# Second attention of a two-layer encoder trunk: all projections first, then the units, then one output projection

## The reference

```python
def chunk_band_mixer(h, w_in, q_g, k_g, rel_table):
    proj = h @ w_in                       # 1024 -> 3 * 1024
    q, k, v = jnp.split(proj, 3, axis=-1) # 16 heads of 64
    q = rmsnorm(q.reshape(B, S, N_HEADS, HEAD_DIM), q_g)
    k = rmsnorm(k.reshape(B, S, N_HEADS, HEAD_DIM), k_g)
    ...
    # per 64-frame chunk: its own chunk and the 8 before it
    logits = jnp.einsum('bqhd,bkhd->bhqk', q_c, k_c) * HEAD_DIM ** -0.5 + bias
    logits = jnp.where(valid, logits, -jnp.inf)
    p = jax.nn.softmax(logits, axis=-1)
    o = jnp.einsum('bhqk,bkhd->bqhd', p, v_c)
```

## Time and profile before

| | |
|---|---|
| median of 3 runs | 3090.85 us (3089.18 to 3092.53) |
| profiled execution: time, span | 3089.12 us, 3087.3 us |
| granted clock of PE, mean | 0.960 |
| PE busy over the span | 2810.6 us, 91% |
| PEld | 2390.3 us, 77% |
| DVE | 1702.2 us, 55% |
| ACT | 1042.0 us, 34% |
| POOL | 790.8 us, 26% |

### The profile page before, as it was taken

How to read it: one execution, slowest core, us unless ns; L and a number is a source line. 1 busy time by engine, 2 the same in 40 slices (tenths; PEclk the granted TensorE clock), 3 DMA queues, 4 the chain that set the end, 5 groups by cost and what they waited for, 6 DMA issues and landing times. The chain is left out here.

```text
span 3087.3 us, 38817 instructions
## 1 busy us (share of the span) xinstructions
PE 2810.6 (91%) x14642; PEld 2390.3 (77%) x14674; DVE 1702.2 (55%) x2824; ACT 1042.0 (34%) x1912; POOL 790.8 (26%) x417
## 2 busy tenths in 40 slices
PE   5879498999899999999888888888887999999999
PEld 4679387888788888888777877777776888888887
DVE  4689766661444444444556555556566544445444
ACT  4567455551322222222333332333334222222221
POOL 2031433302332232322231111121102322232322
PEclk9989699999999999999989999999998999999999
DMA  4010000011111111111010000000001111111111
GB/s 158 1 62 21 21 8 8 5 59 35 68 54 44 48 50 45 54 48 48 36 43 5 29 33 33 33 1 33 13 8 55 55 48 48 41 54 41 54 48 62
DMA packets 36310, 124.09 MB, mean 40 GB/s; under 512 B 3968, under 2 KB 12336, under 8 KB 34384
## 3 DMA queue, kind: packets, MB, share of 16 engines
q1 hardware_dynamic: 36176, 122.29, 11.4%
HBM read 118.03 MB, written 9.49 MB: 41 GB/s over the span
## 5 line engine op out<-in xcount | busy, mean ns | idle before, releaser
L330 PE MATMUL banks<-XH,WH 128*128 128x512 f32 x1408 | 436.2, 391 | 8.2 <-POOL WL L291 6.1
L330 PE MATMUL banks<-XL,WH 128*128 128x512 f32 x1408 | 434.8, 390 | 0.0
L330 PE MATMUL banks<-XH,WL 128*128 128x512 f32 x1408 | 434.6, 390 | 0.0
L291 POOL TENSOR_TENSOR WL<-WR,WH 128x1024 fp32r<-128x1024 f32 x132 | 331.0, 2515 | 370.3 <-ACT WH L245 370.3
L386 DVE TENSOR_TENSOR U<-banks,RB 128x1024 f32<-128x1024 f32 x88 | 107.8, 1225 | 407.4 <-PE banks L330 398.1
L260 ACT ACTIVATE Y<-U,CONVB,CONVW 128x1024 f32<-128x1024 f32 x88 | 109.5, 1245 | 633.0 <-DVE U L386 633.0
L330 PEld LDWEIGHTS banks<-XH,WH 128*128 128x128 f32 x1408 | 265.0, 188 | 64.8 <-POOL WL L291 6.3
L330 PEld LDWEIGHTS banks<-XL,WH 128*128 128x128 f32 x1408 | 265.1, 188 | 55.3
L330 PEld LDWEIGHTS banks<-XH,WL 128*128 128x128 f32 x1408 | 265.1, 188 | 55.3
L376 DVE TENSOR_TENSOR XT<-XT,banks 128x1024 f32<-128x1024 f32 x176 | 214.4, 1218 | 165.2 <-PE banks L346 165.2
L299 POOL TENSOR_TENSOR AL<-Y,AH 128x1024 fp32r<-128x1024 f32 x44 | 105.8, 2405 | 611.3 <-ACT AH L268 611.3
(11 more groups left out here) (217 smaller groups left out, 5624.8 us busy)
## 6 DMA issues: line engine op xcount, KB each, us to landing
WR<-in_ffn SPq DMA_DIRECT2D x132, 512.0 KB, 3.2
QWR<-in_qkv SPq DMA_DIRECT2D x12, 1536.0 KB, 7.4
XT<-in_xT SPq DMA_DIRECT2D x16, 512.0 KB, 6.9
OWR<-in_w_o SPq DMA_DIRECT2D x16, 512.0 KB, 3.7
outT<-XT SPq DMA_DIRECT2D x8, 512.0 KB, 2.6
near<-strip SPq DMA_DIRECT2D x1, 3072.0 KB, 24.7
BB<-near SPq DMA_DIRECT2D x8, 384.0 KB, 5.0
near<-strip SPq DMA_DIRECT2D x1, 2048.0 KB, 15.3
```

The costliest lines, as they stand in the source:

```text
L291: pool.tensor_tensor(WL[:, ch % RING, :], WR[:, ch % RING, :], WH[:, ch % RING, :].bitcast(F32), ALU.subtract).then_inc(w_lo, 1)
L330: mm = pe.matmul(u[:, h * HALF:(h + 1) * HALF], w[:, ch % RING, db * P:(db + 1) * P], x[:, db, h * HALF:(h + 1) * HALF], start=(db == 0 an ...
```

## The change

`attention_phase` is replaced by `band_phase`, which has three parts.

The opening runs the projections of all 64 tiles, in rotation through six banks, with two sets of weights. ScalarE copies each tile from its bank to SBUF, where it stays, and takes the sums of squares with four activations; VectorE makes the variance and, one tile later, normalises queries and keys in place. In the last eight tiles (t = 56 to 63) GpSimd also doubles the columns of tile t - 56 into `DUP`, and PE turns them behind its projection. The tiles need the space of XT, so x is written out to DRAM (`spill`) at the start and read back before the last group's units are done.

The units, 128 in all, have logits three ahead. In the even units of all groups but the last, PE turns the heads of a tile of the next group; in odd units it turns an output. Both use the one bank `TQ`, and `DUP` is single. The bias is blanked by GpSimd.

The close is one output projection over all groups: for each of 8 blocks of features 48 matmuls, two banks in turn, then one addition to XT. Output weights come by columns.

```diff
+def band_phase(nc, c, w_qkv, w_o, near, stage, spill):
...
+        AHEAD = 3
...
+        LG = c.pair[0:2]
         TP = c.bank[4:6]
         OP = c.bank[6]
-        PJ = c.bank[7]
-        DN = [c.pair[0], c.pair[1], c.pair[3]]
+        TQ = c.bank[7]
+        DN = c.pair[0:2]
+        PJ = c.bank[0:6]
...
+        @block.sync
...
+            sp.dma_start(WR[0][:], w_qkv[0]).then_inc(w_landed[0], 16)
+            sp.dma_start(WR[1][:], w_qkv[1]).then_inc(w_landed[1], 16)
+            for db in range(DB):
+                sp.dma_start(spill[:, db, :], c.XT[:, db, :]).then_inc(spilled, 16)
...
+                if k == 7:
+                    sp.wait_ge(pv_ready, 5 * UNITS)
+                    sp.wait_ge(spilled, 16 * DB)
+                    for db in range(DB):
+                        sp.dma_start(c.XT[:, db, :], spill[:, db, :]).then_inc(x_landed, 16)
...
+        @block.scalar
...
+            def take(t):
...
+                act.wait_ge(pj_ready, t + 1)
...
+                act.activation(tile(t), bank[:, 0:PROJ], ACT.Copy, scale=c.RSTD[:, i:i + 1])
...
+                for h in range(NH):
+                    mm = act.activation(JUNK[:, h * HD:(h + 1) * HD], bank[:, h * HD:(h + 1) * HD], ACT.Square, scale=c.RSTD[:, i:i + 1],
+                                        accum_out=SSQ[:, t % 2, h:h + 1])
+                mm.then_inc(taken, 1)
...
+            for t in range(TILES):
+                k, i = divmod(t, TT)
+                take(t)
+                if i in (3, 4) and k + 1 < GROUPS:
+                    weights_high(k + 1, i - 3)
+                if k == GROUPS - 1:
+                    heads_high(i, i)
...
+        @block.gpsimd
...
+            def doubled(t):
+                pool.wait_ge(normed, t + 1)
+                if t >= 1:
+                    pool.wait_ge(turned, round_of_tile(t - 1) + 1)
+                pool.tensor_copy(DUP[:].rearrange("p (h k d) -> p h k d", h=NH, k=2),
+                                 tile(t)[:, 0:NH * HD].rearrange("p (h d) -> p h d", h=NH).unsqueeze(2)
+                                 .to_broadcast([P, NH, 2, HD])).then_inc(dup_ready, 1)
+
+            norm.root(pool)
+            pool.memset(BB[:, :, :, 0:PW - W], 0.0).then_inc(b_blank, 1)
+            weights_low(0, 0)
+            weights_low(0, 1)
+            for t in range(TILES):
+                k, i = divmod(t, TT)
+                pool.wait_ge(var_ready, t + 1)
+                if t >= 2:
+                    pool.wait_ge(normed, t - 1)
+                pool.tensor_tensor(RS[:, t % 2, :], VAR[:, t % 2, :], c.NHALF[:, 0:NH], ALU.pow).then_inc(rs_ready, 1)
+                if i in (4, 5) and k + 1 < GROUPS:
+                    weights_low(k + 1, i - 4)
+                if k == GROUPS - 1:
+                    doubled(i)
...
+            def heads(t, r):
+                pe.wait_ge(dup_ready, t + 1)
+                if r >= 1:
+                    pe.wait_ge(turned_lo, r)
+                for j in range(NH):
+                    mm = pe.transpose(TQ[:, j * P:(j + 1) * P], DUP[:, j * PAIR:(j + 1) * PAIR], c.IDF[:])
+                mm.then_inc(turned, 1)
+
+            def output(o, r):
+                pe.wait_ge(turned_lo, r)
+                pe.wait_ge(mo_ready, o + 1)
+                pe.transpose(TQ[:, 0:P], MO[:, o % 2, :], c.IDF[:]).then_inc(turned, 1)
...
+                    pe.matmul(out, QS[:, h, cols], KH[k % 2][:, h, k0 + a:k0 + b], start=True, stop=False)
+                    mm = pe.matmul(out, QS[rows, h, cols], KL[k % 2][rows, k0 + a:k0 + b], start=False, stop=True)
...
+            for t in range(TILES):
+                project(t)
+                if t >= TILES - TT:
+                    heads(t - (TILES - TT), t - (TILES - TT))
+            pe.wait_ge(taken, TILES)
+            for g in range(AHEAD):
+                logits(g)
+            for g in range(ALL):
+                turn(g)
+                if g + AHEAD < ALL:
+                    logits(g + AHEAD)
+                if tile_of(g) is not None:
+                    heads(tile_of(g), rounds_before(g))
+                if output_of(g) is not None:
+                    output(output_of(g), rounds_before(g))
+                if g >= 1:
+                    values(g - 1)
...
+            finish(0, range(GROUPS - 1), False)
+            output(ALL // 2 - 1, LAST_ROUND)
+            pe.wait_ge(turned_lo, LAST_ROUND + 1)
+            finish(0, range(GROUPS - 1, GROUPS), True)
+            for db in range(1, DB):
+                finish(db, range(GROUPS), True)
...
+        @block.vector
...
+            def heads_low(t, r):
+                k, cols = t // TT, slice(t % TT * P, (t % TT + 1) * P)
+                dve.wait_ge(turned_hi, r + 1)
+                for h in range(2):
+                    lo = slice((1 - h) * HD, (2 - h) * HD)
+                    up = slice(h * HD, (h + 1) * HD)
+                    dve.scalar_tensor_tensor(QS[lo, h, cols], TQ[lo, h * P:(h + 1) * P], c.HGAIN[lo, 2:3],
+                                             QS[lo, h, cols].bitcast(F32), ALU.mult, ALU.subtract)
+                    mm = dve.scalar_tensor_tensor(KL[k % 2][up, cols], TQ[up, (2 + h) * P:(3 + h) * P],
+                                                  c.HGAIN[up, 3:4], KH[k % 2][up, h, cols].bitcast(F32),
+                                                  ALU.mult, ALU.subtract)
+                mm.then_inc(turned_lo, 1)
...
+            for g in range(ALL):
+                k, i, h = place(g)
+                if blocks(i) >= 4:
+                    dve.wait_ge(t_first, g + 1)
+                    dve.tensor_copy(PT[:, g % 2, 0:HALF], TP[0][:]).then_inc(pt_dve, 1)
+                if g + AHEAD < ALL:
+                    row_max(g + AHEAD)
+                if tile_of(g) is not None:
+                    heads_low(tile_of(g), rounds_before(g))
+                if output_of(g) is not None:
+                    output_low(output_of(g), rounds_before(g))
+                if h == 0 and g >= 2:
+                    output(g // 2 - 1)
+                if g % UNITS == UNITS // 2 and k + 1 < GROUPS:
+                    mask(k + 1)
...
-        attention_phase(nc, c, BAND, a["qkv"][4:12], a["w_o"][1], nears[1], 2)
+        band_phase(nc, c, a["qkv"][4:12], a["w_o"][1], nears[1], 2, spill)
```

More of the change, by code:

```diff
@@ L461, in pieces @@
     return [(a, min(a + HALF, n)) for a in range(0, n, HALF)]
-def attention_phase(nc, c, mx, w_qkv, w_o, near, stage=None):
-    L = mx.layer
+def band_phase(nc, c, w_qkv, w_o, near, stage, spill):
+    mx = BAND
     near = near.rearrange("(r h) p n -> r p h n", h=2)
     with ExitStack() as ctx:
-        sem, old = c.signals.open(ctx, f"a{L}")
-        m = Map(nc, c.scratch, c.top)
[L475 to L510, removed]
-        GATE = m.take(f"GATE{L}", [P, 2], F32)
-        SP_ = c.pair[0:2]
@@ L745, in _, with weights_low @@
[L745 to L755 removed]
+            pool.sem_clear(old)
+            def weights_low(k, h):
+                pool.wait_ge(w_hi, 2 * k + h + 1)
+                pool.tensor_tensor(WL[k % 2][:, half(h), :], WR[k % 2][:, half(h), :],
+                                   WH[k % 2][:, half(h), :].bitcast(F32), ALU.subtract).then_inc(w_lo, 1)
@@ new lines, in acts_before, with values @@
+            def acts_before(g):
+                return sum(blocks(place(v)[1]) != 4 for v in range(g))
+            def values(g):
+                k, i, h = place(g)
+                if h == 0 and g >= 2:
+                    pe.wait_ge(mo_ready, g // 2)
+                pe.wait_ge(pt_act, acts_before(g + 1))
+                if firsts_before(g + 1):
+                    pe.wait_ge(pt_dve, firsts_before(g + 1))
+                last = blocks(i) - 1
+                for b in range(last + 1):
+                    mm = pe.matmul(OP[:, h * HD:(h + 1) * HD], PT[:, g % 2, b * P:(b + 1) * P],
+                                   tile(k * TT + i - last + b)[:, (NH + h) * HD:(NH + h + 1) * HD],
+                                   start=(b == 0), stop=(b == last))
+                mm.then_inc(pv_ready, 1)
@@ L1047, in _ @@
+            output(ALL // 2 - 1)
+            output_low(ALL // 2 - 1, LAST_ROUND)
+            dve.wait_ge(x_landed, 16 * DB)
+            for db in range(DB):
+                dve.wait_ge(dn_ready, db + 1)
+                dve.tensor_tensor(c.XT[:, db, :], c.XT[:, db, :], DN[db % 2][:], ALU.add).then_inc(dn_free, 1)
+                if db % 2 == 0 and db >= 2:
+                    squares.add(dve, db - 1)
             squares.add(dve, DB - 1)
```

734 lines of the change are left out of this document (287 added, 447 removed).

## The result

The changed kernel takes 3285.7 us (median of 4 runs, 3271.5 to 3300.3) against 3090.0 (3088.0 to 3092.5) before: ratio 1.064, 95% interval 1.0614 to 1.0666. The forecast of 3068 and its range up to 3110 both missed. The profiled execution took 3271.49 us, its span is 3269.7 (before 3087.3). The other runs lie at the two ends: one more at 3271.6, two at 3300 with a mean granted clock of 0.886 in place of 0.897. In this document a median is over all runs of a kernel, while a ratio and its interval leave out those runs over 1.5% above the fastest of their kernel.

A forecast was written before the change was run, and what follows sets the result against it. PE was taken as the bounding engine, with up to 87 us of idle to win. Opening 324.4, units 360.8 and close 99.9 sum to 785.1 against 807.8, so 3091 - 23 = 3068 us; range 3015 to 3110.

The forecast's parts named there:

- The failed step: Residue (KL) matmuls of the second attention's logits: 64 rows with as many columns, so no gain counted.
- Term 1: Second attention's opening, projections of 64 tiles: 233.0 dense, 2.8 first tile, 88.6 last eight; 324.4 us.
- my 235.8: Opening's first 56 tiles: 56 x 4.16 = 233.0 us dense, plus 2.8 for the first tile.
- the stall: Opening's last eight tiles: PE's head turn waits for GpSimd's doubling; 4.45 us each, above 5.4, or 5.6 without read overlap.
- Term 2: Second attention's units: 4.8 start, seven filled pairs of 46.5, last pair 30.5; 360.8 us.
- the named chain: Filled pairs' rows: head turn, ScalarE split, DVE residues, then reciprocal and output before PE's output turn; 3.6 us.
- Term 3: Closing output projection up to the first FFN matmul: 99.9 us, as in the first attention.
- 43.6 + 3: One filled pair: rows sum to 43.6 us, 3 added for PE's idle in short rows; taken as 46.5.
- C: Units and opening slower: idle in rows keeps PE's clock low, pairs 52; +40 us, 3131; chance 0.20.
- B: Filled pairs in units: waits overlap better, pairs at DVE's and PE's own work, 38; 3008 us; chance 0.18.

The follow-up runs named there:

- experiment 5: Kernel of experiment 1 with GpSimd doubling tile t - 56 ahead of the root of tile t: 3034.4 us, ratio 0.9817.
- experiment 10: Changed kernel with residue matmuls on 128 rows, FFN buffers at their former place and GpSimd's doubling ahead of the root: 3006.3 us, ratio 0.9736.
- experiment 11: Experiment 10 with the new order: VectorE makes output ahead of head residues, TensorE turns an output behind the previous unit's values: 2966.9 us, ratio 0.9602.
- experiment 1: Changed kernel with the units' residue matmuls on all 128 rows instead of 64: 3073.5 us, ratio 0.9953.
- experiment 3: Experiment 1 with both FFN phases' buffers 896 bytes further on, where they stood before the change: 3047.1 us, ratio 0.9859.
- experiment 14: Changed kernel, still on 64 rows, with only the new order of output and residues: 3188.3 us, ratio 1.0366.
- experiment 13: Experiment 11 with its residue matmuls put back on 64 rows: 3031.8 us, ratio 0.9815.
- 4: Changed kernel with GpSimd doubling tile t - 56 ahead of the root of tile t: 3230.8 us, ratio 1.0432.
- experiment 15: Experiment 13 with each 64-row residue matmul issued twice, so its product counts twice: 3064.4 us, ratio 0.9922.

## Why the prediction was wrong, step by step

**The failed step** is the sentence "The KL matmuls use 64 rows and as many columns, so I count no gain". It priced an edit at nothing from below and from above; the trace of before held no matmul of 64 rows, and so nothing excluded a loss. The runs put in its place: 196.4 us in the units (544.8 against 348.4 with 128 rows), 212 us in the medians (3285.7 against 3073.5). With the new order, 35 of such a loss remain at full clock. If they are much the same in the old order, some 160 are the clock; that split is worked out, not measured, as no run of the old order kept the full clock.

**Term 1, the opening**, 319.3 for 324.4. The mechanism was right: eight stalls, each released by GpSimd's DUP. One of them, in the changed kernel's timeline:

```profile
1803.00 0.58 ACT L628 ACTIVATE THIGH<-banks,RSTD 128x384 f32<-128x384 f32 x1 [2.46 <-PE banks L764]
...
1804.80 0.17 DVE L877 TENSOR_SCALAR QVAR<-SSQ 128x4 f32<-128x4 f32 x1 [3.73 <-ACT JUNK L634]
...
1805.05 1.11 POOL L735 TENSOR_TENSOR RS<-QVAR,NHALF 128x4 f32<-128x4 f32 x1 [3.11 <-DVE QVAR L877]
1806.12 0.60 POOL L722 COPY DUP<-TLOW 128x512 f32<-128x512 f32 x1
...
1806.78 1.12 PE L774 MATMUL banks<-IDF,DUP 128*128 128x128 f32 x4 [3.82 <-POOL DUP L722]
```

Idle 3.82 where 4.45 stood: ScalarE's part is 1.80 for 1.95 and the doubling 0.60 for 0.75, close to the lower bound of 0.58. The next such turn starts at 1816.89, a period of 10.1 for 11.3 (10.2 over all eight). Against that the first 56 tiles were some 3 us over my 235.8 (the 57th ends at 1802.8, which makes 239). What I did not see is that the stall needed no new buffer to go: the doubling of tile i depends on nothing of tile 56+i, and ahead of its root it saves 39 us (experiments 5 and 10).

**Term 2, the units**, was right once the rows are put back: 348.4 for 360.8, with 4.8 to the first head turn (4.8 forecast), filled pairs of 44.6 for 46.5, about 31 left for the last pair (30.5), and the waits before the output turn released by DVE MO, at clock 0.96. That the named chain is the bound is shown by experiment 11, which only reorders it: 40.9 us of the units go (347.6 in experiment 10 to 306.7).

**Term 3, the close**, 103.3 for 99.9, and 102.0 in experiment 1.

**What no step had**: the place of the two FFNs' buffers, 26 us. It moved because three constants left the setup; I had priced only the four VectorE operations that fill them, at "under 1 us". With both mended, experiment 3 stands at 3047 for a forecast of 3068.

**Small slips in the working.** The parts of the stall add up to 4.41 and not 4.45, its upper bound without overlapping reads to 6.1 and not 5.6, and 43.6 + 3 is 46.6 and not 46.5. Together they move the forecast by less than 1 us.

**Rivals.** C named the clock and gave it 0.20, but for another reason and far too small: it had idle in every row and priced 40 us. Idle alone did not do it: the kernel with 67 us of waits for MO kept 0.95, and the one with 12 fell to 0.50. (At half clock the waits shrink by themselves, so the 12 us are also a consequence.) Waits do help to bring the clock down where 64-row matmuls are there: the new order, worth 39 us with 128 rows (experiment 11 against 10), is worth 97 with 64 (experiment 14 against the changed kernel), and 173 where the stalls are gone too (experiment 13 against 4, the 26 us of the place taken off). B's pairs of 38 came true, nearly, only with the order changed (39).

**What stays open.** The units with 64-row matmuls have two lasting levels. Full-row work, fewer changes, fewer 64-row columns and fewer waits each make the upper one more frequent; more 64-row work in the kernel without waits did not hold it down (experiment 15: 3064 and not over 3200). What exactly starts and ends a stretch at the lower level no run isolates, and runs of one kernel differ by up to 92 us in it (experiment 13).

The Trainium skill, page "TensorE: Matmul & The Clock Gate", section HAM oscillation, has idle gaps between bursts as the cause of a throttled clock. The stalled opening agrees (0.85 in 1795:1879). The units do not fit it alone, with TensorE 98% busy at 0.51, and the measurement decides.

## What to carry to other kernels

A matmul on 64 rows with the same columns is not free beside one on 128: in such a sequence count 0.3 us of TensorE's time for each inserted one, of which 0.16 to 0.26 came through to the total here, and watch the granted clock, for a stretch that is 98% busy at 0.50 hides half its speed. Where an edit changes the shape of a matmul that the trace doesn't have, leave room above zero in its price. Before adding buffers to a stalled chain, look for an operation in each engine's list that stands behind another it does not need.

## What the hardware showed that I had not expected

- The shortest high-part matmul (128 columns) between 64-row ones takes 305 ns in place of 220, at the upper clock, although its own rows are the same.
- Adding 192 full-row matmuls made the kernel 146 us faster (3286 to 3140), by the clock.
- 896 bytes in the place of SBUF buffers change the pace of dense matmuls by 1.6% (434 against 441 in 100 us, 393 against 389 ns), at the full clock. Which of the buffers matters wasn't tried.
